# The state tiles' imaginary product: from the vector engine to GpSimd, and its place in GpSimd's queue

## The chip, the cores and the metric

One core of one Trainium2 chip runs the whole program. The metric is the device time of one execution in microseconds, the median of several runs; lower is better. The core has five engines with a queue each: TensorE (PE: matmuls, and PEld for its weight loads), VectorE (DVE), ScalarE (ACT), GpSimd (POOL) and SyncE (SP), which here only issues loads. The engines work in parallel and meet at semaphores. Matmul results go into eight banks of PSUM; everything else the engines share lies in SBUF.

## The reference, cut to what matters

The reference runs two transformer-like blocks of two layers each on 512 positions of width 1024. The change lies in the second block, in the state space part of each layer:

```python
a_bar = jnp.exp(lam * dt)
b_bar = ((a_bar - 1.0) / lam)[..., None] * b_mat
bu = jnp.einsum("bsgh,gph->bsgp", uf.astype(jnp.complex64), b_bar)
...
a_seq = jnp.broadcast_to(a_bar, (1, seq) + a_bar.shape)
_, states = lax.associative_scan(combine, (a_seq, bu), axis=1)
c_mat = lax.complex(c_re.astype(jnp.float32), c_im.astype(jnp.float32))
y = jnp.real(jnp.einsum("bsgp,ghp->bsgh", states, c_mat))
```

There are 16 groups of 64 complex states, so 1024 complex recurrences over 512 positions. Beside it each layer computes a spatial gate, and a differential attention with 4 heads of 2 softmaxes.

## The kernel before, in words

Everything is in float32. The complex recurrence is made real: inputs are turned by the angle of the position so that both parts become plain scans with a real decay, the scans run, and their results are turned back. The 1024 states are eight tiles of 128 partitions, by 512 positions. Turning by an angle takes three multiplications with tables (cos, sin - cos, sin + cos) and a few additions.

For layer `l` and tile `i` the steps are these.

- TensorE, `state_in(i)` (L1221): three products of the layer's input, each into a bank.
- VectorE, `turn_in(i)` (L2531): each bank times a table, into `turned[0..2]`.
- GpSimd (L2030, L2031): `turned[1]` becomes the sum and `turned[2]` the difference with `turned[0]`.
- VectorE, `scan(i)` (L2541, L2543): the scans, into `z_re` and `z_im`.
- GpSimd (L2027): `z_sum = z_re + z_im`.
- VectorE, `turn_out(i)` (L2552, L2553, L2555): `z_re`, `z_im` and `z_sum` times a table each, into `out_parts[1]`, `[2]` and `[0]`. Before it writes, it waits until the product of tile `i - 1`, which reads the same buffers, is in its bank.
- TensorE, `state_out(i)` (L1229): the product of `out_parts` with the output matrices, summed in one bank, called `("yp", l, i)`.
- VectorE, `add_y(i)` (L2499 for tiles 0 and 4, L2504 for the others): adds that bank to the result and so drains it.

Each queue is written out by hand and executed in order. TensorE's holds, for tile `i`: `state_in(i + 1)`, `state_out(i - 1)`, then three steps of the attention (L795 scores, L813 transposes, L825 products with the values). VectorE's holds: `scan(i)`, `turn_in(i + 1)`, in tile 0 the spatial gate (L2577), one attention step (L2201, L2210, L2212, L2218 or L2222), `turn_out(i)`, `add_y(i - 1)`, two more attention steps. GpSimd's holds: L2027 of tile `i`, then L2030 and L2031 of tile `i + 1`. ScalarE has the attention's exponentials and copies (L1486, L1498).

TensorE takes the eight banks in turn, so before it fills one it waits until what was in it eight fills ago is drained; this is how a late `add_y` holds it. SyncE loads tables and matrices of each tile from DRAM into three buffers in turn (L1301, L1303): the load for tile `i + 3` waits until the product of tile `i` is in its bank, and `state_in(i + 3)` waits for the load.

The feed-forward network that follows uses L1786 and L1788 on GpSimd (weights split in two parts), and L2628 and L2083 among others on VectorE.

Of the kernel before, what the change touches and what calls it, by code (L numbers as in the profile page):

```python
# [11 lines left out]
ALU = mybir.AluOpType  # L12
# [33 lines left out]
S5_BUFS = 3  # L46
# [87 lines left out]
def build(nc, A, out, upto=99):  # L134
    ctx = ExitStack()
    with ctx:
# [44 lines left out]
        def region(base, *dims):  # L181
            n = int(np.prod(dims))
            ap = arena[:, base:base + n]
            if len(dims) == 2:
                return ap.rearrange("p (a b) -> p a b", a=dims[0])
            return ap
# [80 lines left out]
        s5_tabs = [region(9216 + 3 * T * b, 3, T) for b in range(S5_BUFS)]  # L267
        mats0 = cst[:, CONST["cosm"][0]:CONST["cosm"][0] + 2 * S5_MATS].rearrange("p (m n) -> p m n", m=6)
        s5_mats = [mats0] + [region(13824 + 2 * S5_MATS * b, 6, P) for b in range(S5_BUFS - 1)]
        z_re, z_im, z_sum = (xnT[:, i, :] for i in range(3))  # L270
        turned = [xnT[:, 3 + i, :] for i in range(3)]
        out_parts = [xnT[:, 6, :], xnT[:, 7, :], region(16128, T)]
# [64 lines left out]
        def s5(name):  # L337
            at, w = S5_AT[name]
            return sp_[:, at:at + w]
# [4 lines left out]
        def S(name):  # L344
            if name not in made:
                made[name] = ctx.enter_context(nc.semaphore(name))
            return made[name]
# [18 lines left out]
        def filled_sem(key):  # L366
            return (over_filled if over(key) else bank_filled)[number[key] % BANKS], number[key] // BANKS + 1

        def bank(key):
            return psum[number[key] % BANKS]  # L370

        def wait_filled(eng, key):
            eng.wait_ge(*filled_sem(key))
            return bank(key)
# [4 lines left out]
        def wait_drained(eng, key):  # L379
            eng.wait_ge(drained_sem(key), number[key] // BANKS + 1)  # L380
# [168 lines left out]
        def _(pe):  # L549
            def claim(key):  # L550

                n = tiles[over(key)]
                tiles[over(key)] += 1
                assert key not in number, key
                number[key] = n
                if n >= BANKS:
                    pe.wait_ge(drained_sem(key), n // BANKS)
                return psum[n % BANKS]

            def fill(ins, key):  # L560
                ins.then_inc(filled_sem(key)[0], 1)
# [603 lines left out]
            with pe.If(n_tokens > CAP):  # L1165
                for i in range(BANKS):
                    n = tiles[False] - 1 - i
# [10 lines left out]
            for l in range(L2):  # L1178
# [45 lines left out]
                def state_out(i):  # L1224

                    ps = claim(("yp", l, i))
                    pe.wait_ge(S("out_parts_ready"), 8 * l + i + 1)
                    for m in range(3):
                        ins = pe.matmul(ps[:, :], s5_mats[i % S5_BUFS][:, 5 - m, :], out_parts[m], start=m == 0,  # L1229
                                        stop=m == 2)  # L1230
                    fill(ins, ("yp", l, i))
# [537 lines left out]
        def _(pool):  # L1769
# [122 lines left out]
            for t in range(NT):  # L1892
                for a in range(2):
                    i = a * NT + t
# [19 lines left out]
            for q in range(S5_ROUNDS):  # L1914
                l = q // 2
# [50 lines left out]
            for l in range(L2):  # L1966
                for half in range(2):
# [5 lines left out]
                    for k in range(9):  # L1973
                        n = 1 << k
# [20 lines left out]
            for a in range(2):  # L1995
                for t in range(NT):
                    i = a * NT + t
# [6 lines left out]
            for l in range(L2):  # L2004

                if l:
                    wait_drained(pool, ("up", f"ffn2_{l - 1}", KF - 1, 1))
                pool.dma_start(wn, A["gmlp_w_s_2"][l].rearrange("h i j -> i h j")).then_inc(S("gmlp_in"), 16)
                pool.dma_start(vgain, A["gmlp_v_g_2"][l:l + 1, :].broadcast_to([P, 256])).then_inc(S("gmlp_in"), 16)
                for i, name in enumerate(("lambda_q1_2", "lambda_k1_2", "lambda_q2_2", "lambda_k2_2")):  # L2010
                    pool.dma_start(lamrow[:, i, :], A[name][l:l + 1, :].broadcast_to([P, 64])).then_inc(S("gmlp_in"), 16)
                pool.dma_start(subg, A["subln_g_2"][l:l + 1, :].broadcast_to([P, P])).then_inc(S("gmlp_in"), 16)
                pool.wait_ge(S("gmlp_in"), 16 * 7 * (l + 1))
                pool.memset(wn[0:64, :, 64:128], 0.0).then_inc(S("wn_ready"), 1)
                if l == 0:
                    pool.wait_ge(S("results_added"), 2 * NT)
                split(f"in{l}")
                split(f"qk{l}", 6)
                rotary(groups2(l), f"g2_{l}", lambda l=l: split(f"qk{l}", 2))

                for i in range(-1, 8):
                    n = 8 * l + i
                    if i >= 0:
                        pool.wait_ge(S("scan_done"), n + 1)
                        if n:
                            pool.wait_ge(S("out_parts_ready"), n)
                        pool.tensor_tensor(z_sum, z_re, z_im, ALU.add).then_inc(S("z_sum_ready"), 1)  # L2027
                    if i < 7:
                        wait_drained(pool, ("bu", l, i + 1, 0))
                        pool.tensor_tensor(turned[1], turned[0], turned[1], ALU.add).then_inc(S("bu_turned"), 1)  # L2030
                        pool.tensor_tensor(turned[2], turned[0], turned[2], ALU.subtract).then_inc(S("bu_turned"), 1)  # L2031

                wait_filled(pool, ("mt", f"m2_{l}", NT - 1, 1))
                pool.wait_ge(S("y_split"), 2 * (l + 1))
                split(f"out2_{l}")
                if upto <= 6 + 2 * l:
                    return
                split(f"ff{l}")
                if upto <= 7 + 2 * l:
                    return  # L2040
# [3 lines left out]
        def _(dve):  # L2044
# [461 lines left out]
            for l in range(L2):  # L2506
# [26 lines left out]
                def scan(i):  # L2533

                    n = 8 * l + i
                    rb = s5("r")[:, n:n + 1].broadcast_to([P, T])
                    if n:
                        dve.wait_ge(S("out_parts_ready"), n)
                        dve.wait_ge(S("z_sum_ready"), n)
                    dve.wait_ge(S("bu_turned"), 2 * n + 1)  # L2540
                    dve.tensor_tensor_scan(z_re, rb, turned[1], 0.0, ALU.mult, ALU.add)  # L2541
                    dve.wait_ge(S("bu_turned"), 2 * n + 2)
                    dve.tensor_tensor_scan(z_im, rb, turned[2], 0.0, ALU.mult, ALU.add).then_inc(S("scan_done"), 1)  # L2543

                def turn_out(i):

                    n = 8 * l + i
                    tabs = s5_tabs[i % S5_BUFS]
                    dve.wait_ge(S("scan_done"), n + 1)
                    if i:  # L2550
                        wait_filled(dve, ("yp", l, i - 1))
                    dve.tensor_tensor(out_parts[1], z_re, tabs[:, 1, :], ALU.mult)  # L2552
                    dve.tensor_tensor(out_parts[2], z_im, tabs[:, 2, :], ALU.mult)  # L2553
                    dve.wait_ge(S("z_sum_ready"), n + 1)
                    dve.tensor_tensor(out_parts[0], z_sum, tabs[:, 0, :], ALU.mult).then_inc(S("out_parts_ready"), 1)  # L2555

# [52 lines left out]
                for j in range(KF):  # L2609
                    n = up2[0]  # L2610
# [55 lines left out]
```

## Time and profile before

| | us |
|---|---|
| median of 3 runs | 3069.35 (3067.13 to 3070.07) |
| the profiled execution | 3073.82 |
| its span, first to last instruction | 3072.0 |
| TensorE busy | 2920.0 (95%) |
| GpSimd busy | 1605.2 (52%) |
| VectorE busy | 1083.7 (35%) |
| ScalarE busy | 709.7 (23%) |

Busy times are averages over stages with different limits. The state tiles take only a small part of the span: those of the first layer lie at about 1843 to 1938 us, those of the second at 2528 to 2618 us. Matmuls overlap, so a busy TensorE is not one at its peak. In lists by time, a row has its start, its length, engine, line, operation, what it writes and reads, and in brackets the idle time of the engine before it with what ended that. A row's length includes a wait of the instruction for anything that the semaphores don't show.

### The profile page before, as it was taken

Reading aid. Unit: us, or ns where it says so; the run is one execution under the profiler, and the core shown is the slowest. Engines: PE = TensorE matmul, PEld = TensorE weight load, DVE = VectorE, ACT = ScalarE, POOL = GpSimd, SP = SyncE. Lnnn points to the kernel's source line nnn. Section 1 sums busy time; section 2 is a strip of 40 time slices with the busy share of each in tenths; the row PEclk is TensorE's granted clock in tenths of the full one; section 3 lists DMA queues with packets and bytes.
Section 4 is the critical chain, followed back from the end, with each engine's and each line's share of the span. In section 5 each row is a group of like instructions: output and inputs, shape, how many; then the busy total and the mean of one; then the engine's idle time right before and its main releaser. Section 6 shows DMA issues by size and latency. Waiting matters only on the chain.

```text
span 3072.0 us, 38813 instructions
## 1 busy us (share of the span) xinstructions
PE 2920.0 (95%) x14757; PEld 2381.5 (78%) x14757; DVE 1083.7 (35%) x2145; ACT 709.7 (23%) x1735; POOL 1605.2 (52%) x1687
## 2 busy tenths in 40 slices
PE   6999999999999899999999898799999988899999
PEld 3545888888878799999999764588888764688887
DVE  1026643313255200000001238447264148357273
ACT  3135752101110111111110222432022222432020
POOL 0121027767778210107784543278788643378786
PEclk9999999999999899999999998899999989899999
DMA  6260013233442389999999303223333203133331
GB/s 184 61 186 25 15 29 97 89 108 95 124 122 91 96 240 265 263 261 267 299 301 309 111 31 114 63 83 93 106 93 106 79 31 136 45 94 96 102 93 52
DMA packets 543191, 388.07 MB, mean 126 GB/s; under 512 B 31178, under 2 KB 493221, under 8 KB 542488
## 3 DMA queue, kind: packets, MB, share of 16 engines
q1 hardware_dynamic: 523728, 327.85, 37.6%
q0 software_dynamic: 12832, 41.22, 4.0%
q10 hardware_dynamic: 6440, 16.44, 1.5%
q8 instruction: 121, 1.98, 0.3%
q14 instruction: 70, 0.57, 0.1%
HBM read 345.12 MB, written 40.80 MB: 126 GB/s over the span
## 4 chain that ended last, share of the span: by engine, by line
PE 88%; DVE 4%; ACT 3%; issue 2%; DMA 1%; SPq 1%; ACTq 1%; POOL 0%; another core or an unknown queue 0%; DVEq 0%; POOLq 0%
PE bank L593 17%; PE bank L594 17%; PE bank L595 17%; PE bank L728 15%; PE bank L1147 6%; PE bank L825 3%; PE bank L795 2%; PE bank L1221 1%; PE bank L813 1%; PE bank L1229 1%; PE bank L782 1%; PE bank L768 1%; DMA ring<-in_moe_w_down 1%; SPq L1286 1%; PE bank L891 1%
## 5 line engine op out<-in xcount | busy, mean ns | idle before, releaser
L1788 POOL TENSOR_TENSOR unit_parts<-ring,unit_parts 128x512 fp32r<-128x512 f32 x580 | 804.2, 1387 | 48.3
L1786 POOL TENSOR_SCALAR unit_parts<-ring 128x512 fp32r<-128x512 f32 x580 | 425.4, 734 | 538.4 <-PE bank L595 322.6
L593 PE MATMUL bank<-x_hi,unit_parts 128*128 128x512 f32 x1408 | 557.0, 396 | 16.5 <-DVE x L2234 10.3
L594 PE MATMUL bank<-x_lo,unit_parts 128*128 128x512 f32 x1408 | 550.6, 391 | 0.0
L595 PE MATMUL bank<-x_hi,unit_parts 128*128 128x512 f32 x1408 | 550.4, 391 | 0.0
L728 PE MATMUL bank<-arena,ring 128*128 128x160 f32 x2816 | 386.6, 300 | 3.5 <-ACT arena L1617 3.5
L728 PEld LDWEIGHTS bank<-arena,ring 128*128 128x128 f32 x2816 | 384.4, 191 | 3.9 <-ACT arena L1617 3.8
L593 PEld LDWEIGHTS bank<-x_hi,unit_parts 128*128 128x128 f32 x1408 | 265.7, 189 | 75.7 <-DVE x L2234 11.5
L593 PE MATMUL bank<-unit_parts,hid_parts 128*128 128x512 f32 x784 | 308.6, 394 | 9.2 <-DVE hid_parts L2256 9.2
L594 PEld LDWEIGHTS bank<-x_lo,unit_parts 128*128 128x128 f32 x1408 | 265.8, 189 | 57.0 <-issue 2.9
L595 PEld LDWEIGHTS bank<-x_hi,unit_parts 128*128 128x128 f32 x1408 | 265.8, 189 | 56.1
L594 PE MATMUL bank<-unit_parts,hid_parts 128*128 128x512 f32 x784 | 306.8, 391 | 0.0
L595 PE MATMUL bank<-unit_parts,hid_parts 128*128 128x512 f32 x784 | 306.7, 391 | 0.0
L2298 DVE TENSOR_TENSOR arena<-bank,arena 128x160 f32<-128x160 f32 x88 | 28.6, 325 | 567.3 <-PE bank L728 561.2
L1887 POOL TENSOR_TENSOR arena<-arena 128x1024 f32<-128x1024 f32 (+9 forms) x48 | 69.7, 1452 | 265.8 <-ACT arena L1662 265.2
L1147 PE MATMUL bank<-arena,ring 128*128 128x160 f32 x1408 | 195.7, 302 | 5.4 <-DMA ring<-in_moe_w_down 5.4
L1147 PEld LDWEIGHTS bank<-arena,ring 128*128 128x128 f32 x1408 | 193.7, 192 | 6.0 <-issue 5.6
L2234 DVE TENSOR_TENSOR x<-bank,x 128x512 f32<-128x512 f32 x80 | 55.2, 690 | 371.0 <-PE bank L595 371.0
L593 PEld LDWEIGHTS bank<-unit_parts,hid_parts 128*128 128x128 f32 x784 | 148.1, 189 | 40.8 <-DVE hid_parts L2256 10.0
L1755 ACT ACTIVATE arena<-arena,vec 128x512 f32<-128x512 f32 x88 | 71.9, 817 | 464.4 <-DVE arena L2616 464.4
L595 PEld LDWEIGHTS bank<-unit_parts,hid_parts 128*128 128x128 f32 x784 | 148.1, 189 | 31.4
L594 PEld LDWEIGHTS bank<-unit_parts,hid_parts 128*128 128x128 f32 x784 | 148.1, 189 | 30.3
(311 smaller groups left out, 3665.2 us busy)
## 6 DMA issues: line engine op xcount, KB each, us to landing
ring<-in_moe_w_gate SPq DMA_DIRECT2D x88, 512.0 KB, 6.6
ring<-in_moe_w_up SPq DMA_DIRECT2D x88, 512.0 KB, 7.3
ring<-in_moe_w_down SPq DMA_DIRECT2D x64, 704.0 KB, 5.6
ring<-in_w_up SPq DMA_DIRECT2D x88, 512.0 KB, 5.1
ring<-in_w_down SPq DMA_DIRECT2D x16, 1024.0 KB, 5.1
ring<-in_od_w_in SPq DMA_DIRECT2D x24, 512.0 KB, 4.8
s_stream<-arena POOLq DMA_DIRECT2D x12, 1024.0 KB, 9.6
arena<-s_stream SPq DMA_DIRECT2D x16, 768.0 KB, 4.3
```

What stands on the lines that cost most here:

```text
L593: pe.matmul(ps, a[0], b[0], start=start, stop=False)
L594: pe.matmul(ps, a[0], b[1], start=False, stop=False)
L595: return pe.matmul(ps, a[1], b[0], start=False, stop=stop)
L728: ins = pe.matmul(ps[rows_at:rows_at + m, 0:n], w[:, k * width + at:k * width + at + m], src[:, k, :], start=k == 0, stop=k == KD - 1)
L795: ins = pe.matmul(ps[:, 0:k.shape[1]], u["q"](t), k, start=k is ks[0], stop=k is ks[-1])
L825: ins = pe.matmul(ps[:, 0:u["vw"]], pT_buf[0:w, j % 2, kt * P:kt * P + P], u["v"](kt, w), start=kt == 0, stop=kt == kts - 1)
L1147: ins = pe.matmul(ps[:, (m - m0) * CAP:(m - m0 + 1) * CAP], w[:, k * P:(k + 1) * P], hidE[:, k, :], start=k == 0, stop=k == KE - 1)
L1755: act.activation(acc[:, 2 * a + n % 2, :], unscaled[:, a, :], ACT.Identity, scale=vcol("conv_w_2", 132 * l + 88 + f), bias=vcol("conv_b_2" ...
L1786: pool.tensor_scalar(hi, raw, 1.0, 1.0, ALU.mult, ALU.mult).then_inc(S("units_rounded"), 1)
L1788: pool.tensor_tensor(lo, raw, hi.bitcast(F32), ALU.subtract).then_inc(S("units_split"), 1)
L1887: tt = lambda o, a, b, op: link(pool.tensor_tensor(o, a, b, op))
L2234: drain(dve.tensor_tensor(xs, ps[:, :], xs, ALU.add), key)
```

## The change

The multiplication of `z_im` by its table leaves VectorE's `turn_out` and goes into GpSimd's queue, between the sum L2027 and the two additions of the next tile. It takes the wait for tile `i - 1`'s product along (VectorE keeps its own). A new semaphore, `im_turned`, counts it. TensorE waits for it before `state_out`, VectorE before the next tile's scan overwrites `z_im`.

```diff
                     ps = claim(("yp", l, i))
                     pe.wait_ge(S("out_parts_ready"), 8 * l + i + 1)
+                    pe.wait_ge(S("im_turned"), 8 * l + i + 1)
...
                         pool.tensor_tensor(z_sum, z_re, z_im, ALU.add).then_inc(S("z_sum_ready"), 1)
+                        if i:
+                            wait_filled(pool, ("yp", l, i - 1))
+                        pool.tensor_tensor(out_parts[2], z_im, s5_tabs[i % S5_BUFS][:, 2, :], ALU.mult)\
+                            .then_inc(S("im_turned"), 1)
...
                         dve.wait_ge(S("z_sum_ready"), n)
+                        dve.wait_ge(S("im_turned"), n)
...
                     dve.tensor_tensor(out_parts[1], z_re, tabs[:, 1, :], ALU.mult)
-                    dve.tensor_tensor(out_parts[2], z_im, tabs[:, 2, :], ALU.mult)
                     dve.wait_ge(S("z_sum_ready"), n + 1)
                     dve.tensor_tensor(out_parts[0], z_sum, tabs[:, 0, :], ALU.mult).then_inc(S("out_parts_ready"), 1)
```

Line numbers of the changed kernel differ. On GpSimd L2027 becomes L2028, the new multiplication is L2031, L2030 and L2031 become L2035 and L2036. On VectorE the scans are L2547 and L2549, `turn_in` L2536, `turn_out` L2558 and L2560, `add_y` L2504 and L2509. TensorE's `state_out` is L1230; `state_in` and the attention keep their lines.

The queue of GpSimd before, tiles 1 and 2 of the first layer (`bank_drained4` is the drain of the first product of the next tile; `xnT` is the buffer that holds the turned and scanned parts):

```order
L2027 TENSOR_TENSOR xnT<-xnT 128x512 [waits out_parts_ready,scan_done]
L2030 TENSOR_TENSOR xnT<-xnT 128x512 [waits bank_drained4]
L2031 TENSOR_TENSOR xnT<-xnT 128x512
L2027 TENSOR_TENSOR xnT<-xnT 128x512 [waits out_parts_ready,scan_done]
L2030 TENSOR_TENSOR xnT<-xnT 128x512 [waits bank_drained0]
L2031 TENSOR_TENSOR xnT<-xnT 128x512
```

and the same two tiles in the changed kernel (`bank_filled7` and `bank_filled3` are the products of tiles 0 and 1):

```order
L2028 TENSOR_TENSOR xnT<-xnT 128x512 [waits out_parts_ready,scan_done]
L2031 TENSOR_TENSOR arena<-xnT,arena 128x512 [waits bank_filled7]
L2035 TENSOR_TENSOR xnT<-xnT 128x512 [waits bank_drained4]
L2036 TENSOR_TENSOR xnT<-xnT 128x512
L2028 TENSOR_TENSOR xnT<-xnT 128x512 [waits out_parts_ready,scan_done]
L2031 TENSOR_TENSOR arena<-xnT,arena 128x512 [waits bank_filled3]
L2035 TENSOR_TENSOR xnT<-xnT 128x512 [waits bank_drained0]
L2036 TENSOR_TENSOR xnT<-xnT 128x512
```

The multiplication and its wait now stand ahead of both additions of the next tile.

The queue of VectorE before, tile 2 of the first layer, from the second scan to the addition of tile 1's product (`bank_filled3` is that product):

```order
L2543 SCALAR_TENSOR_TENSOR xnT<-s5small,xnT 128x512 [waits bu_turned]
...
L2201 ISA arena,small<-bank,cst 128x512 [waits bank_filled4,probs_ready]
L2201 ISA small 128x1
L2222 SCALAR_TENSOR_TENSOR arena<-bank,small,arena 128x128 [waits bank_drained7,bank_filled7]
L2552 TENSOR_TENSOR xnT<-xnT,arena 128x512 [waits bank_filled3,scan_done]
L2553 TENSOR_TENSOR arena<-xnT,arena 128x512
L2555 TENSOR_TENSOR xnT<-xnT,arena 128x512 [waits z_sum_ready]
L2504 TENSOR_TENSOR arena<-arena,bank 128x512 [waits bank_drained7,bank_filled3]
```

and in the changed kernel:

```order
L2549 SCALAR_TENSOR_TENSOR xnT<-s5small,xnT 128x512 [waits bu_turned]
...
L2206 ISA arena,small<-bank,cst 128x512 [waits bank_filled4,probs_ready]
L2206 ISA small 128x1
L2227 SCALAR_TENSOR_TENSOR arena<-bank,small,arena 128x128 [waits bank_drained7,bank_filled7]
L2558 TENSOR_TENSOR xnT<-xnT,arena 128x512 [waits bank_filled3,scan_done]
L2560 TENSOR_TENSOR xnT<-xnT,arena 128x512 [waits z_sum_ready]
L2509 TENSOR_TENSOR arena<-arena,bank 128x512 [waits bank_drained7,bank_filled3]
```

Two operations are left between the attention's step and the addition, and VectorE's own wait for `bank_filled3` stays at the first of them.

## Rows read from the trace of the kernel before

**Rows 1.** The page: the span, and busy time of each engine.
```profile
span 3072.0 us, 38813 instructions
...
PE 2920.0 (95%) x14757; PEld 2381.5 (78%) x14757; DVE 1083.7 (35%) x2145; ACT 709.7 (23%) x1735; POOL 1605.2 (52%) x1687
```

**Rows 2.** Stretch, first layer, tiles 2-7: us; busy PE, PEld, DVE, ACT, POOL; clock; DMA.
```profile
1871.80:1936.60 64.80, 56.03 (x232) 30.91 (x231) 52.77 (x117) 16.47 (x50) 20.12 (x16) 0.95 0.40 142
```

**Rows 3.** The chain of waits in the first layer's tiles: start us, us, what.
```profile
1877.47 0.60 DVE xnT L2555
...
1908.38 6.46 DMA arena<-s_stream
...
1921.79 0.63 PE bank L795 x4
...
1925.17 0.60 DVE xnT L2555
```

**Rows 4.** Groups by line and shape, GpSimd (count, busy us, mean ns).
```profile
L2031 POOL TENSOR_TENSOR xnT<-xnT 128x512 f32<-128x512 f32 x16 | 20.4, 1272 | 0.0
...
L1805 POOL TENSOR_TENSOR arena<-arena,cst 128x512 f32<-128x512 f32 x16 | 17.5, 1092 | 55.8 <-DVE arena L2180 55.8
```

**Rows 5.** The list by time, tile 3 of the first layer.
```profile
1885.65 0.32 SPq L1301 DMA_DIRECT2D arena<-s_stream  x1
...
1887.33 0.83 DVE L2552 TENSOR_TENSOR xnT<-xnT,arena 128x512 f32<-128x512 f32 x1
...
1888.69 0.68 DVE L2555 TENSOR_TENSOR xnT<-xnT,arena 128x512 f32<-128x512 f32 x1
...
1890.02 0.49 PE L825 MATMUL bank<-arena 128*128 128x128 f32 x2 [1.17 <-DVE arena L2504]
...
1890.97 2.84 PE L1221 MATMUL bank<-arena 128*128 128x512 f32 x6 [0.46 <-DMA arena<-s_stream]
```

**Rows 6.** The list by time, tiles 2, 5, 6 and 7 of the first layer.
```profile
1873.93 0.32 SPq L1301 DMA_DIRECT2D arena<-s_stream  x1
...
1876.19 0.68 DVE L2552 TENSOR_TENSOR xnT<-xnT,arena 128x512 f32<-128x512 f32 x1
...
1877.39 0.68 DVE L2555 TENSOR_TENSOR xnT<-xnT,arena 128x512 f32<-128x512 f32 x1
...
1914.88 4.34 PE L1221 MATMUL bank<-arena 128*128 128x512 f32 x6 [1.27 <-DMA arena<-s_stream]
...
1923.88 0.68 DVE L2552 TENSOR_TENSOR xnT<-xnT,arena 128x512 f32<-128x512 f32 x1
...
1925.08 0.68 DVE L2555 TENSOR_TENSOR xnT<-xnT,arena 128x512 f32<-128x512 f32 x1
...
1933.24 0.68 DVE L2552 TENSOR_TENSOR xnT<-xnT,arena 128x512 f32<-128x512 f32 x1
...
1934.44 0.69 DVE L2555 TENSOR_TENSOR xnT<-xnT,arena 128x512 f32<-128x512 f32 x1
```

**Rows 7.** The list by time, GpSimd and VectorE in a feed-forward network.
```profile
2741.31 0.62 POOL L1786 TENSOR_SCALAR unit_parts<-ring 128x512 fp32r<-128x512 f32 x1 [0.20 <-PE bank L595]
...
2747.68 1.60 POOL L1788 TENSOR_TENSOR unit_parts<-ring,unit_parts 128x512 fp32r<-128x512 f32 x1
...
2748.16 1.66 DVE L2628 TENSOR_TENSOR whole<-arena 128x512 f32<-128x512 f32 x1
...
2749.25 1.06 POOL L1786 TENSOR_SCALAR unit_parts<-ring 128x512 fp32r<-128x512 f32 x1
...
2749.75 1.10 DVE L2083 TENSOR_TENSOR hid_parts<-whole,hid_parts 128x512 fp32r<-128x512 f32 x1
```

**Rows 8.** The list by time, second layer: TensorE after tiles 3 and 5.
```profile
2574.14 2.84 PE L1221 MATMUL bank<-arena 128*128 128x512 f32 x6 [0.40 <-DMA arena<-s_stream]
...
2596.62 2.74 PE L1221 MATMUL bank<-arena 128*128 128x512 f32 x6
```

**Rows 9.** Busy times by stretch, first layer behind tile 5.
```profile
1915.00:1917.50 2.50, 2.50 (x3) 1.05 (x4) 1.31 (x2) 0.00 (x0) 1.11 (x1) 0.50 1.04 404
```

## The prediction

> **What bounds the kernel now.** I read the page first. The span is 3072.0 us and TensorE is busy for 95% of it, VectorE for 35%, GpSimd for 52% [rows 1], so an edit on VectorE and GpSimd can only count where TensorE waits for one of them. The edit sits in the two loops over state tiles, eight tiles for each layer of the second block. The busy times by stretch show them: tiles 2 to 7 of the first layer fill 64.80 us, with VectorE busy 52.77 us and TensorE 56.03 us of them [rows 2]. There VectorE is nearly as full as TensorE.
>
> Next comes the chain of waits through this loop [rows 3]. The reader is to see two kinds of link. In some tiles it runs through VectorE: the turning out (L2553, L2555), the addition of the last tile's product (L2504), and then TensorE, which wants the bank that this addition drains. In others it runs through the load of a later tile's tables, which starts when the product of an earlier tile is in its bank (L1229) and takes some 5 us. In the first layer loads end it after tiles 1, 3 and 5, VectorE in tiles 2, 4, 6 and 7; in the second VectorE has tile 5 as well. So VectorE's turning out lies on the path in nine of the sixteen tiles, and just behind it in others.
>
> **What the change removes.** Sixteen VectorE multiplications (L2553). A row of the kind shows 0.68 us, but they follow one another every 0.6 us (L2552 at 1933.24, L2555 two steps later at 1934.44 [rows 6]). If nothing else moved, the nine tiles on VectorE's path would give 9 x 0.6 = 5.4 us.
>
> **What it adds.** Sixteen multiplications of 128x512 on GpSimd. The nearest rows are L1805, the same operation on the same shape with both operands read in full, 1.09 us, and the additions around it, 1.27 us [rows 4]. I take 1.09, since that is a multiplication; successive operations there start some 0.05 us earlier than the row's length, so a step is 1.04 for it and 1.22 for an addition. GpSimd idles most of the loop, so the time itself costs nothing. What matters is where it lands.
>
> Before, GpSimd's three operations of a tile (the sum L2027, then L2030 and L2031 on the next tile) end just before VectorE begins to turn out. The new one waits until the previous tile's product is in its bank, and L2030 and L2031 queue behind it. In tile 3 of the first layer the product is there at 1885.65, when the queue that waits for the same event issues its load [rows 5]. The multiplication then runs 1885.67 to 1886.71, and L2030 and L2031 follow where before they were over at 1887.6. VectorE arrives at L2552 at 1887.33 [rows 5], in the middle of L2030.
>
> **The price of meeting.** In the second layer's feed-forward network VectorE's L2628, both inputs in SBUF, shows 1.66 us where one alone takes about 0.6: it ends 0.54 us after GpSimd's L1788. The GpSimd operation behind it (L1786) shows 1.06 us against about 0.62 undisturbed, and L2083, next on VectorE, 1.10 [rows 7]. So two such operations never run at once, and with both queues full they take turns, one and one. By the Trainium skill (SBUF — State Buffer, who interferes with whom) a VectorE instruction with two SBUF inputs and a GpSimd one that reads SBUF exclude each other for the whole instruction, and whichever comes first goes first; this trace agrees with the exclusion (1.66 us). That rule speaks against this change: without it the sum would be the gain of 5.4 us above, with it the loss below.
>
> **The sum, tile by tile** (first layer, shift of the start of L2555 against its own row).
> - Tile 3: L2552 waits for L2030's end, 1887.93, and runs to 1888.53; now L2031 has its turn, to 1889.75; L2555 starts then, before at 1888.69 [rows 5]. That is +1.06. TensorE waited 0.46 us more for a load here [rows 5], so 0.60 comes through.
> - Tile 2: the product is there at 1873.93, L2552 is ready at 1876.19 and finds L2030 just ending; it runs to 1876.84, L2031 to 1878.06; L2555 before 1877.39 [rows 6]. +0.67, all on the path.
> - Tiles 4 and 5: taken as tile 3, whose pattern they repeat, +1.06. Tile 4 has no load behind it and passes all on. After tile 5 TensorE waits 1.27 us for a load anyway [rows 6]: 0.
> - Tile 6: the product comes late, at 1921.79, when TensorE goes on to L795 [rows 3]. L2552, ready at 1923.88, runs from 1924.07 to 1924.67, L2031 to 1925.90, L2555 before 1925.08 [rows 6]: +0.82.
> - Tile 7: nothing follows the multiplication on GpSimd, and it is over when L2552 starts at 1933.24. L2555 loses the step before it: -0.60.
> - Tiles 0 and 1: 0. In tile 0 TensorE's slow matmuls hide it, in tile 1 a load does, and L2555 moves by -0.2 at most.
>
> First layer: 0.67 + 0.60 + 1.06 + 0 + 0.82 - 0.60 = +2.55 us. The second layer repeats the pattern. Its waits differ in two places: 0.40 us for the load after tile 3, and none after tile 5 [rows 8]. 0.67 + 0.66 + 1.06 + 1.06 + 0.82 - 0.60 = +3.67. Together +6.2 us.
>
> Edits that cost nothing. TensorE's new wait for the multiplication precedes a matmul that comes a whole tile, 10 us, later. VectorE's new wait before the scan is met by then too. L2031 of tile 3 ends at 1889.75 and its reader, the scan of tile 4, starts at 1891.5 or later. That cover of over 1.7 us is what the loop would lose first if the queue grew. The load queue waits for the same banks as before.
>
> **The clock.** Longer waits of TensorE can drop its clock. After the load wait of 1.27 us behind tile 5 it was granted 0.50 (1.2 of 2.4 GHz) in 1915.0 to 1917.5, and L1221 showed 4.34 us instead of the 2.84 of tile 3 [rows 5, 6, 9]: +1.5 us. The waits of tile 3, 1.17 us for VectorE and 0.46 for a load, did not bring a fall: L1221 behind them shows 2.84. The change stretches the waits for VectorE in tiles 2 to 4 of both layers, six of them, by 0.7 to 1.1 us, to about 2. Between no fall and six (0 to +9.0) I take two, +3.0: that lies nearer to the row of tile 3, which brought none, and part of a slow stretch can fall into a wait and cost nothing.
>
> Sum against the profiled execution: 3072.0 + 6.2 + 3.0 = 3081.2 us of span. That execution took 3073.82 us, 4.5 above the median of the three runs, 3069.35. The same difference on the median gives 3078.6 us.
>
> **Rivals.**
> - *VectorE keeps its place.* If its two turning operations ran back to back in spite of GpSimd waiting, L2555 would lose no turn: it would start 0.6 us after L2552: 1876.84 against 1877.39 is -0.55 in tile 2, 1888.53 against 1888.69 is -0.16 in tiles 3 to 5, 1924.67 against 1925.08 is -0.41 in tile 6, and -0.60 in tile 7. On the path that makes -0.55 - 0.16 - 0.41 - 0.60 = -1.7 us in the first layer and -1.9 in the second (tile 5 too): 3065.7. For it speaks that the two have nothing between them. Against it stands the turn-taking of rows 7, where L2083 was next in line and still let L1786 through.
> - *The relief counts and the meeting does not*, the other side. If the two queues only seldom met, because the additions were early or the wait for the bank ended earlier, the nine tiles on the path would keep their 0.6: 3069.35 - 5.4 = 3064.0. The point of decision is whether L2030 has ended when L2552 is ready; by the rows it has not in tiles 3, 4 and 6.
> - *The clock falls every time.* 3069.35 + 6.2 + 9.0 = 3084.6. For it speaks the fall behind tile 5; against it, that the new waits stand alone, with busy stretches between.
> - *The queue reaches the scan.* If L2031 ended over 1.7 us later than worked out, the scan of the next tile would wait and everything with it, about 1 us in each of 12 tiles: 3069.35 + 6.2 + 12 = 3087.6. The rows leave room.
>
> **How the numbers follow.** About 0.2%, 6.1 us, is what a measurement of this kernel can tell from no change. Forecast (turns taken, none to three falls, 3075.5 to 3080.1) 0.58; every or nearly every fall 0.14; VectorE keeps its place 0.14; relief 0.10; scan reached 0.04. The forecast's low end, +6.2 without any fall, lies at the bound, so a fifth of it counts as the same. Slower by over 0.2%: 0.46 + 0.14 + 0.04 = 0.64. Same: 0.12 + 0.14 + most of relief (-5.4 is inside the bound) 0.06 = 0.32. Faster: 0.04. The range leaves out the relief and the scan's case: 3065.5 to 3086.5 us.
>
> **What would show it.** Right: sixteen rows of the new L2031 on GpSimd near 1.09 us, starting as the product's bank fills; L2558 often longer than 0.68 us; L2036 with rows of about 1.9 us, having waited a turn; L2560 over 1.2 us after L2558 in tiles 2 to 6; TensorE's waits for L2509 longer by about 1 us. Wrong: L2560 0.6 us behind L2558 throughout, which is the first rival, or TensorE's waits for it shorter than before, which is the second. Any wait of L2547 for GpSimd would show the last rival. Were the clock's term wrong, the loop alone would say so: its granted clock against 0.95 in tiles 2 to 7 [rows 2].

## The result and the profile after

The changed kernel takes 3088.2 us in the median of 5 runs (3086.66 to 3094.16), the kernel before 3070.07 (3067.13 to 3074.57): a ratio of 1.0061, 95% interval 1.0049 to 1.0074. It is slower by some 18 us. The forecast had the sign and not the size: 3078.6, with a range that ended at 3086.5. The profiled execution took 3086.96 us.

The page of the changed kernel, against [rows 1]: 13.1 us more span, and GpSimd busy 25.9 us more. VectorE gave away sixteen multiplications and is busy 5.0 us longer all the same. The last row is TensorE's granted clock in 40 slices of the span, 77 us each. The two loops lie at slices 24 to 26 and 33 to 35; six slices show 8 there, where the kernel before has four.

```profile
span 3085.1 us, 38828 instructions
...
PE 2929.3 (95%) x14757; PEld 2387.7 (77%) x14757; DVE 1088.7 (35%) x2129; ACT 710.1 (23%) x1735; POOL 1631.1 (53%) x1703
...
PEclk9999999999999899999999988899999988899999
```

Tile 3 of the first layer, listed by time, against [rows 5]:

```profile
1884.47 0.32 SPq L1302 DMA_DIRECT2D arena<-s_stream  x1
1884.53 1.27 POOL L2031 TENSOR_TENSOR arena<-xnT,arena 128x512 f32<-128x512 f32 x1 [1.84 <-PE bank L1230]
...
1885.75 1.28 POOL L2035 TENSOR_TENSOR xnT<-xnT 128x512 f32<-128x512 f32 x1
...
1886.15 1.42 DVE L2558 TENSOR_TENSOR xnT<-xnT,arena 128x512 f32<-128x512 f32 x1
...
1886.97 1.72 POOL L2036 TENSOR_TENSOR xnT<-xnT 128x512 f32<-128x512 f32 x1
...
1887.50 1.75 DVE L2560 TENSOR_TENSOR xnT<-xnT,arena 128x512 f32<-128x512 f32 x1
...
1889.16 0.67 DVE L2509 TENSOR_TENSOR arena<-arena,bank 128x512 f32<-128x512 f32 x1
...
1889.89 0.72 PE L825 MATMUL bank<-arena 128*128 128x128 f32 x2 [2.23 <-DVE arena L2509]
...
1890.41 4.24 PE L1221 MATMUL bank<-arena 128*128 128x512 f32 x6
```

This is the meeting that was forecast. GpSimd's three operations start as the product's bank fills. VectorE's first (L2558) holds on until L2035 is over, GpSimd's L2036 until L2558 is over, VectorE's second (L2560) until L2036 is over, and the waits stand as length in the rows: 1.42, 1.72 and 1.75 us for work of 0.6, 1.2 and 0.6. From the queue's load to the end of `turn_out`'s last operation it was 1889.37 - 1885.65 = 3.72 us before, and is 1889.25 - 1884.47 = 4.78 now: +1.06, as worked out. TensorE's wait went from 1.17 to 2.23 us.

What comes behind the wait is the other part. The same six matmuls of L1221 took 2.84 us before and take 4.24 now. Stretches of tile 3 in the changed kernel (us; busy PE, PEld, DVE, ACT, POOL; clock; DMA):

```profile
1885.00:1890.00 5.00, 2.77 (x22) 2.08 (x21) 4.12 (x5) 1.23 (x4) 3.70 (x3) 1.00 0.67 236
1890.00:1892.50 2.50, 2.50 (x5) 1.42 (x6) 2.43 (x10) 1.25 (x5) 0.00 (x0) 0.50 0.00 0
1892.50:1895.00 2.50, 2.50 (x6) 0.99 (x5) 1.44 (x3) 0.00 (x0) 1.23 (x1) 0.82 0.00 0
```

The clock falls to its lower level, 1.2 GHz, as TensorE comes back from its wait, and has risen again before the last stretch ends. Much the same happens in tiles 1 to 6 of both layers. TensorE's rows behind its waits, first layer, tiles 1, 2, 4, 5, 6 and 7 in turn:

```profile
1863.02 1.22 PE L825 MATMUL bank<-arena 128*128 128x128 f32 x4 [2.29 <-DVE arena L2504]
1864.03 3.83 PE L1221 MATMUL bank<-arena,cst 128*128 128x512 f32 x6
1875.89 0.48 PE L795 MATMUL bank<-arena 64*128 64x128 f32 x2 [1.86 <-DVE arena L2509]
1878.49 3.37 PE L1221 MATMUL bank<-arena 128*128 128x512 f32 x6
...
1902.67 1.13 PE L795 MATMUL bank<-arena 64*128 64x512 f32 x2 [1.88 <-DVE arena L2509]
1905.28 3.63 PE L1221 MATMUL bank<-arena,cst 128*128 128x512 f32 x6
1916.99 1.82 PE L825 MATMUL bank<-arena 128*128 128x128 f32 x8 [2.38 <-DVE arena L2504]
1918.61 3.79 PE L1221 MATMUL bank<-arena 128*128 128x512 f32 x6
1930.43 1.16 PE L795 MATMUL bank<-arena 64*128 64x384 f32 x2 [2.50 <-DVE arena L2509]
1939.63 0.60 PE L825 MATMUL bank<-arena 128*128 128x128 f32 x3 [0.52 <-DVE arena L2509]
```

Before, L1221 showed 2.84, 2.74, 2.84, 2.74 and 4.34 us behind the waits of tiles 1 to 5, so one of five was slow; now all five are. Behind tile 6 none follows, but L795 takes 1.16 us for 0.91 before. And no wait for a load is left: all are for `add_y`.

For the sum over both loops I take the time from the start of the scan of tile 0 to that of tile 7 in each layer. Before and after (columns as above):

```profile
1847.49:1928.23 80.74, 69.50 (x275) 40.08 (x275) 68.46 (x158) 18.59 (x60) 26.38 (x21) 0.90 0.36 129
2529.15:2608.83 79.68, 69.22 (x271) 40.18 (x271) 68.46 (x158) 18.80 (x60) 26.38 (x21) 0.89 0.37 131
```

```profile
1842.56:1932.93 90.37, 75.98 (x271) 44.47 (x271) 71.30 (x150) 18.91 (x60) 37.99 (x28) 0.82 0.32 115
2532.01:2622.40 90.39, 75.96 (x271) 44.44 (x271) 71.30 (x151) 18.91 (x60) 38.01 (x28) 0.82 0.33 115
```

Together 160.4 us before and 180.8 after, +20.3; with tile 7's turning out, which lost its multiplication, the loops grew by 19.1 us. They hold the whole loss. TensorE is busy 13.2 us more in them with the same matmuls, and that is the clock, not the wait: idle time does not count as busy.

### The profile page after: what moved, and what is told of

Same layout as the page of the kernel before. It is cut to its first block, busy times and chain, and to the rows that moved or that the text cites. A ratio compares the mean times of both kernels' runs of the same rounds, so it can differ in the third digit from the quotient of the medians.

```text
span 3085.1 us, 38828 instructions
## 1 busy us (share of the span) xinstructions
PE 2929.3 (95%) x14757; PEld 2387.7 (77%) x14757; DVE 1088.7 (35%) x2129; ACT 710.1 (23%) x1735; POOL 1631.1 (53%) x1703
## 4 chain that ended last, share of the span: by engine, by line
PE 88%; DVE 4%; ACT 3%; issue 2%; DMA 1%; SPq 1%; ACTq 0%; POOL 0%; another core or an unknown queue 0%; DVEq 0%; POOLq 0%
PE bank L593 17%; PE bank L595 17%; PE bank L594 17%; PE bank L728 15%; PE bank L1147 6%; PE bank L825 3%; PE bank L795 2%; PE bank L1221 2%; PE bank L813 1%; PE bank L1230 1%; PE bank L782 1%; PE bank L768 1%; DMA ring<-in_moe_w_down 1%; SPq L1287 1%; DVE xnT L2560 1%
## 6 DMA issues: line engine op xcount, KB each, us to landing
s_stream<-arena POOLq DMA_DIRECT2D x12, 1024.0 KB, 10.1
```

## The experiments

All were timed beside the kernel before, and each ratio is to its time there (3070.8 to 3072.5 us in the median on the experiments' chips, 3070.07 beside the changed kernel). "Loops" is the sum of the two stretches just defined, "clock" the granted clock from the scan of tile 2 to that of tile 7, first and second layer, both from one profiled execution.

| kernel | median us | ratio (95%) | loops us | clock |
|---|---|---|---|---|
| before | 3070.8 to 3072.5 | 1 | 160.4 | 0.97, 0.98 |
| changed | 3088.20 | 1.0061 (1.0049 to 1.0074) | 180.8 | 0.88, 0.88 |
| e1 two buffers | 3073.09 | 0.9997 (0.9984 to 1.0009) | 158.7 | 0.98, 0.94 |
| e2 last in the queue | 3084.48 | 1.0036 (1.0023 to 1.0049) | 170.5 | 0.94, 0.90 |
| e3 longer VectorE | 3105.91 | 1.0099 (1.0083 to 1.0114) | 189.7 | 0.86, 0.86 |
| e4 changed, filled | 3074.76 | 1.0005 (0.9997 to 1.0014) | 164.4 | 1.00, 1.00 |
| e5 relief alone | 3063.66 | 0.9977 (0.9965 to 0.9989) | 156.8 | 0.95, 0.98 |
| e6 addition alone | 3102.17 | 1.0101 (1.0082 to 1.0119) | 195.6 | 0.85, 0.85 |
| e7 before, filled | 3063.27 | 0.9971 (0.9959 to 0.9983) | 156.5 | 1.00, 1.00 |
| e8 two buffers, filled | 3060.28 | 0.9964 (0.9954 to 0.9975) | 154.3 | 1.00, 1.00 |
| e9 longer VectorE, filled | 3083.23 | 1.0036 (1.0024 to 1.0049) | 170.5 | 1.00, 1.00 |
| e10 changed, half filled | 3076.59 | 1.0011 (0.9998 to 1.0023) | 164.8 | 1.00, 0.99 |
| e11 two buffers, filled more | 3067.40 | 0.9983 (0.9971 to 0.9995) | 154.9 | 1.00, 1.00 |

What lies outside the loops differs from execution to execution: the first scan starts anywhere from 1840.4 us (e4) to 1850.9 (e11), in kernels that are alike up to there. So the loops of one execution say more of a mechanism than the medians do, and the intervals bound what the medians say. How often the clock falls is read from one execution of each kernel too. The granted clock of the whole span, known for every timed execution, goes the same way: in the mean 0.970 for the kernel before, 0.968 for the changed one, 0.969 for e1 and e2, 0.971 for e5, 0.964 and 0.965 for e3 and e6, 0.972 to 0.974 for the six filled ones.

**e1, the meeting taken away.** Two buffers for the imaginary part, so that GpSimd multiplies right behind its sum, long before VectorE's turning out. `state_out` reads the two in turn (not shown here).

```diff
+        im_parts = [region(16128, T), region(16640, T)]
...
-                        if i:
-                            wait_filled(pool, ("yp", l, i - 1))
-                        pool.tensor_tensor(out_parts[2], z_im, ..., ALU.mult)
+                        if i >= 2:
+                            wait_filled(pool, ("yp", l, i - 2))
+                        pool.tensor_tensor(im_parts[i % 2], z_im, ..., ALU.mult)
```

> The changed kernel with two buffers for the imaginary product, so that GpSimd's multiplication follows its sum at once and does not wait for the last tile's product. Theory A (the loss is the place: GpSimd's additions pushed into VectorE's turning out, which then gives up turns, and TensorE's clock behind the longer waits): the three operations of GpSimd end at most 0.5 us later than before, L2560 starts as in the kernel before or 0.6 us sooner, granted clock in tiles 2 to 7 back near 0.95; 3066 to 3070 us, ratio to the kernel before 0.999 to 1.000. Rival B (the work on GpSimd itself costs, wherever it stands): still some 18 us slower, ratio 1.005 to 1.006.

3073.09 us, 0.9997: the 18 us are gone, as expected. VectorE's two operations follow each other in 0.6 us (tile 2, first layer), and TensorE's wait is 0.64 us where it was 1.24 before and 1.86 in the changed kernel:

```profile
1877.71 0.68 DVE L2559 TENSOR_TENSOR xnT<-xnT,arena 128x512 f32<-128x512 f32 x1
1878.31 0.69 DVE L2561 TENSOR_TENSOR xnT<-xnT,arena 128x512 f32<-128x512 f32 x1
1878.91 0.68 DVE L2510 TENSOR_TENSOR arena<-arena,bank 128x512 f32<-128x512 f32 x1
1879.64 0.48 PE L796 MATMUL bank<-arena 64*128 64x128 f32 x2 [0.64 <-DVE arena L2510]
```

So the loss hangs on where GpSimd's work lands, not on its amount and not on the new semaphore, which both stayed. The relief brings little against the kernel before here: 1.7 us in the loops.

**e2, behind both additions.** The multiplication and its wait moved behind GpSimd's L2035 and L2036 of the changed kernel; the same lines leave their old place (not shown here).

```diff
                         pool.tensor_tensor(turned[2], turned[0], turned[2], ALU.subtract).then_inc(S("bu_turned"), 1)
+                        if i:
+                            wait_filled(pool, ("yp", l, i - 1))
+                        pool.tensor_tensor(out_parts[2], z_im, ..., ALU.mult).then_inc(S("im_turned"), 1)
```

> The changed kernel with GpSimd's multiplication, and its wait for the last tile's product, behind both additions of the next tile. Theory A: the additions end as before, but the multiplication itself now meets the turning out: one turn of 1.2 us between the two VectorE operations, less the 0.6 saved: about +0.7 us in tiles 2 to 6 (5 us in all), and part of the clock's cost; 3077 to 3084 us, ratio 1.002 to 1.005. Rival C (the harm is the additions arriving late for the next scan, not the meeting): back to 3064 to 3070 us.

1.0036, inside what was expected. VectorE's two operations now meet one GpSimd operation, the multiplication, where they met two; TensorE's wait in tile 3 is 1.64 us, between the 1.17 of before and the 2.23 of the changed kernel, and half of what the loops had lost stays (10.1 of 20.3 us). That the additions come late for the next scan, the rival here, is out: they are back in their place and the kernel is still slower.

**e3, only VectorE's work made longer.** The kernel before, with `turn_out`'s second multiplication issued three times, twice into buffers that nobody reads. GpSimd's queue is as before.

```diff
                     dve.tensor_tensor(out_parts[2], z_im, tabs[:, 2, :], ALU.mult)
+                    for at in (16640, 15360)[:2]:
+                        dve.tensor_tensor(region(at, T), z_im, tabs[:, 2, :], ALU.mult)
```

> The kernel before, with two more multiplications of z_im into scratch on VectorE in each turning out (1.2 us per tile), GpSimd untouched. It lengthens TensorE's wait for VectorE in tiles 2 to 6 by the same 1 us or so as the change, without any meeting. Clock theory (a longer wait lowers TensorE's clock, whatever makes it): about +13 us of waits on the path and +9 to +12 us of slower matmuls: 3090 to 3096 us, granted clock in tiles 2 to 7 near 0.88, L1221 3.4 to 4.3 us in place of 2.8. Rival (the clock fell for another reason, such as GpSimd's traffic): +13 us only, 3083 us, clock stays near 0.95.

3105.91 us, more than either theory had. It shows without GpSimd's part that a later `add_y` alone brings the clock down (0.86) and costs more than the work that delays it: 1.2 us of VectorE's work for each of twelve waiting tiles are 14.4 us, and the loops grew by 29.3.

**e4, the changed kernel with its waits filled.** TensorE's wait for the bank comes first; what is filled is the wait for `add_y` one claim later, with products of the identity with itself in the bank that is about to be used and is overwritten after.

```diff
+            key_at = {}
...
                 if n >= BANKS:
                     pe.wait_ge(drained_sem(key), n // BANKS)
+                key_at[n] = key
+                late = key_at.get(n + 1 - BANKS, ("",))
+                if late[0] == "yp":
+                    for _ in range(8 if late[2] in (1, 3, 5) else 6 if late[2] in (0, 2, 4) else 0):
+                        pe.matmul(psum[n % BANKS][:, 0:P], c("ident"), c("ident"), start=True, stop=True)
                 return psum[n % BANKS]
```

> The changed kernel, with TensorE kept busy where it waits for VectorE's addition: in the bank claimed just before that wait it multiplies the identity by itself, 8 times in tiles 2, 4 and 6 and 6 times in tiles 1, 3 and 5 (1.3 to 1.8 us), before the real products overwrite it. Clock theory: granted clock in tiles 2 to 7 over 0.95, L1221 back to 2.7 to 2.9 us, time 8 to 12 us under the changed kernel: 3076 to 3080 us. Rival (the slower clock costs nothing, the matmuls would wait anyway): 3088 us or more, since the added products delay some real ones.

3074.76 us, better than expected: 8 to 12 us under the changed kernel were forecast, and by the ratios (1.0005 against 1.0061) it is some 17. This separates the two parts of the loss, since VectorE and GpSimd do just what they do in the changed kernel. They still take turns (tile 3):

```profile
1882.35 1.72 POOL L2043 TENSOR_TENSOR xnT<-xnT 128x512 f32<-128x512 f32 x1
1882.76 1.50 PE L564 MATMUL bank<-cst 128*128 128x128 f32 x12
1882.86 1.75 DVE L2567 TENSOR_TENSOR xnT<-xnT,arena 128x512 f32<-128x512 f32 x1
...
1885.26 0.49 PE L832 MATMUL bank<-arena 128*128 128x128 f32 x2 [0.89 <-DVE arena L2516]
1885.59 2.74 PE L1228 MATMUL bank<-arena 128*128 128x512 f32 x6
```

L564 is the filling. `add_y` comes as late as ever (the turning out ends 4.77 us after the load queue's issue at 1879.84, in the changed kernel 4.78), but `state_in` (L1228 here) is back at 2.74 us, and the loops are 16.4 us shorter than the changed kernel's. Work that computes nothing gave the time back.

**e5, the relief alone.** The kernel before without VectorE's multiplication. The imaginary part of the state outputs is left out of the computation; its buffer is zeroed once per layer.

```diff
-                    dve.tensor_tensor(out_parts[2], z_im, tabs[:, 2, :], ALU.mult)
```

> The kernel before with VectorE's multiplication of the imaginary part left out and nothing put in its place; its buffer is zeroed once per layer, so the imaginary part of the state outputs is left out of the computation. It prices the relief alone. By the sum of the prediction nine tiles on VectorE's path give 0.6 us each: -5.4 us, ratio 0.998 (3066 to 3068 where the kernel before takes 3072.5). If the clock's loss grows with the length of TensorE's waits, as the larger-than-expected loss of the longer turning out (+33 us for +19 us of VectorE work) suggests, shorter waits also give back some of the slow matmuls of tiles 0 and 5: -7 to -11 us, ratio 0.9965 to 0.998. Rival, that loads end the waits wherever VectorE does not: -1 to -3 us, ratio 0.9990 to 0.9997.

0.9977, -7.1 us on the ratio, with -3.6 in the loops and some -1.2 more in the two last tiles. The prediction's -5.4 lies between; the case in which loads take over everywhere (-1 to -3) is out by the ratio's interval.

**e6, the addition alone.** The kernel before keeps VectorE's multiplication and gets GpSimd's too, into a spare buffer, with the waits of the change.

```diff
                         pool.tensor_tensor(z_sum, z_re, z_im, ALU.add).then_inc(S("z_sum_ready"), 1)
+                        if i:
+                            wait_filled(pool, ("yp", l, i - 1))
+                        pool.tensor_tensor(region(16640, T), z_im, ..., ALU.mult).then_inc(S("im_turned"), 1)
```

> The kernel before, VectorE's multiplication kept, with GpSimd's new multiplication added at the place and with the waits of the change, into a buffer that nobody reads. It prices what the change adds, without its relief. Turns: VectorE has three operations where the changed kernel has two, so its last one ends some 0.6 us later than there, about 1.7 us later than before in tiles 2 to 6; as the clock falls with such waits (the changed kernel lost 16 us to it at +1.1 us per tile), the time is beyond the changed kernel's: +24 to +34 us, ratio 1.008 to 1.011. If the meeting costs nothing and the change's loss came from elsewhere (the moved buffer, the new waits of TensorE alone), this kernel is at 1.000 to 1.002.

1.0101, inside the range for turns. Tile 3, in which GpSimd's multiplication started at 1890.42:

```profile
1892.05 1.41 DVE L2558 TENSOR_TENSOR xnT<-xnT,arena 128x512 f32<-128x512 f32 x1
...
1893.38 1.75 DVE L2559 TENSOR_TENSOR arena<-xnT,arena 128x512 f32<-128x512 f32 x1
1895.05 0.68 DVE L2561 TENSOR_TENSOR xnT<-xnT,arena 128x512 f32<-128x512 f32 x1
```

The turning out ends 5.31 us after that start, in the changed kernel 4.72 us after it (1884.53 to 1889.25): the multiplication that VectorE kept, 0.59 us. So the change as a whole is an addition that costs more and a relief that gives some of it back. The two do not simply add up: without GpSimd's addition the relief is worth 3.6 us of loops (e5), with it 195.6 - 180.8 = 14.8, twice the 7.2 of VectorE's work in twelve tiles, since the clock comes up with it (0.85 to 0.88).

**e7 and e8, the kernel before and e1 filled.** The filling of e4 with five and four products instead of eight and six, once in the kernel before and once in e1.

> The kernel before, with idle multiplications of TensorE (five for odd tiles, four for even, identity by identity into a bank that is claimed already) ahead of each of its waits for the addition of tiles 0 to 5. Clock theory: the kernel before loses something to the clock too (L1221 4.34 behind tile 5, 4.73 in tile 0), and filling the waits gives part of it back: -2 to -6 us, ratio 0.998 to 0.9995, granted clock of the loops 0.99 to 1.00. If the fillers help only by hiding something else in the changed kernel, or cost what they give, 1.000 to 1.001 here.

> The changed kernel with two buffers for the imaginary part (GpSimd's multiplication right behind its sum, ahead of the meeting) and TensorE's waits filled as in the run on the kernel before. The candidate that should beat both kernels. With two buffers alone the ratio was 0.9997 and the granted clock of the loops 0.98 and 0.94; with the clock at 1.00, 3 to 6 us of slower matmuls go: ratio 0.998 to 0.999, 3066 to 3069 where the kernel before takes 3072.5. If the two repairs do not add up, 0.9995 to 1.0005.

Both came out better than expected: 0.9971 and 0.9964, with the clock at 1.00. The kernel before had been losing to its clock too, 3.9 us of its loops (its four falls are told of below). e8 beats both kernels, by 10.5 us and by about 28; the two repairs add up in the loops (-1.7 from the buffers, -3.9 from the filling, -6.1 together). That medians gain 4 to 5 us more than the loops is not explained; such a part is within what executions differ by outside of them.

**e9, e3 filled.** Eleven and ten products.

> The run with the longer turning out on VectorE (ratio 1.0099 without filling, loops at a granted clock of 0.86) with TensorE's waits filled as well: eleven idle multiplications for odd tiles, ten for even, 0.25 us each, about as long as its waits of 3 us. It splits that kernel's loss into waits and clock. Its TensorE was busy 8.0 us longer than before in tiles 2 to 7 of each layer. If that is the clock's doing, filling gives 16 us back: 1.004 to 1.006, granted clock 1.00 in the loops. If the loss is VectorE's work alone, with TensorE's slow rows hidden beside it, it stays at 1.009 to 1.010.

1.0036 against 1.0099, more given back than expected. Of e3's loops 189.7 - 170.5 = 19.2 us were clock, and 170.5 - 156.5 = 14.0 the longer work itself when both are at full clock, close to the 14.4 of twelve tiles at 1.2.

**e10, the changed kernel half filled.** Four and three products.

> The changed kernel with half the filling: four idle multiplications for odd tiles and three for even, about 1.0 and 0.75 us of waits of 1.9 to 2.5. Full filling gave 1.0005, none 1.0061. If the clock's loss falls in proportion to the idle time that is left, 1.003 to 1.0035; if what counts is whether the idle time that is left is about as short as that of the kernel before (0.8 to 1.3 us, which cost it little), most comes back: 1.0005 to 1.002, granted clock of the loops over 0.96. If half the filling brings nothing, 1.005 to 1.006.

1.0011. The return is not proportional: half the filling does what the whole one did (loops 164.8 against 164.4). In tile 3 of this kernel 0.83 us are filled and 1.56 us of the wait are left, and the clock stays up:

```profile
1890.84 0.83 PE L564 MATMUL bank<-cst 128*128 128x128 f32 x6
...
1893.35 0.49 PE L832 MATMUL bank<-arena 128*128 128x128 f32 x2 [1.56 <-DVE arena L2516]
1893.67 2.74 PE L1228 MATMUL bank<-arena 128*128 128x512 f32 x6
```

**e11, e8 filled more.** Seven and six products.

> The best kernel so far (two buffers, filled by five and four, ratio 0.9964) with seven and six, 1.75 and 1.5 us, longer than most of its waits. If fillers past the wait's length delay TensorE, 0.3 to 0.5 us in each of twelve tiles, minus what loads end anyway: ratio 0.9970 to 0.9985. If the wait for the addition is longer than the records show, or the clock has something left to give, it stays at 0.996 to 0.9968.

0.9983, in the range for a delay, but the loops do not bear it out: 154.9 us against 154.3 of e8, where a delay in every tile would be 4 to 6. The two intervals touch (0.9971 to 0.9995, 0.9954 to 0.9975). Whether more filling costs anything stays open; it brings nothing. The profiled execution of e11 came to its first scan 8.4 us later than that of e8, ahead of any filling.

## Why the prediction was wrong in size, point by point

- **GpSimd's multiplication**, taken as 1.09 us: 1.27 in all sixteen rows, like the additions. It cost the sum nothing: in tile 3 the turns still end 4.78 us after the bank is filled, as worked out, since the turns behind it were shorter than taken: 0.54 us for L2558 (0.60), 1.12 for L2036 (1.22), 0.56 for L2560 (0.68).
- **The turns, tile by tile**: right. TensorE's waits in the first layer grew by 1.86 - 1.24 = 0.62 in tile 2 (0.67 forecast), 1.06 in tile 3 (1.06), 1.88 - 0.82 = 1.06 in tile 4 (1.06), 2.50 - 1.67 = 0.83 in tile 6 (0.82). To price them without the clock, compare the filled kernels: e4 - e7 = 164.4 - 156.5 = 7.9 us of loops. The forecast's terms without tile 7's, which lies behind the stretch, are 3.15 + 4.27 = 7.4. Tile 5 agrees as well: 1.33 + 1.27 us of waits became 2.38 in the first layer (0 forecast), 1.33 became 2.38 in the second (1.06). By the Trainium skill (SBUF — State Buffer, who interferes with whom) the two kinds of instruction exclude each other for their whole length; rows of 1.72 and 1.75 us for 1.2 and 0.6 us of work agree again.
- **The count of tiles on VectorE's path**: nine was one short. In the second layer no load ends the wait of tile 1; the chain runs through L2555 (2548.53, 0.60 us) and L2499 to L825 there too (its row stands below), which makes ten tiles and a relief of 6.0 us. It changes the forecast by 0.2 us at most, since the meeting moves tile 1 by no more.
- **The clock: the step that failed.** It is "I take two, +3.0". The changed kernel lost 180.8 - 164.4 = 16.4 us to its clock and the kernel before 160.4 - 156.5 = 3.9, so the change added 12.5 us. I had counted six waits that might fall, and two that would: tiles 1 to 6 of both layers, twelve waits, all have a slow stretch. They are not all alike, L1221 shows 3.37 to 4.26 us for 2.74, and a slow stretch also holds rows of L825 (1.22 us behind tile 1 for 0.71 in e4), which I had not counted. The highest price I gave, +9.0 for six falls at 1.5, was too low for the same reasons. The falls do not go with longer waits alone: tile 1's wait got shorter, from 2.47 to 2.29 and 2.30 us, and has a slow stretch in both layers now, where it had one before.
- **Where the reading went wrong**: I took the fall behind tile 5 [rows 6, 9] for the only one and for the effect of a single wait of 1.27 us, and tile 3's wait of 1.17 as proof that others are harmless. I looked at L1221 alone. Behind tile 6 no L1221 follows, and there the kernel before falls too, after one wait of 1.67 us for `add_y`, in both layers (clock 0.50 here, 0.53 in the second); and behind tile 5 it was two waits. List by time, the last two rows from tile 1 of the second layer, then a stretch behind tile 6 of the first:

```profile
1912.44 1.16 PE L825 MATMUL bank<-arena 128*128 128x128 f32 x8 [1.33 <-DVE arena L2499]
1914.88 4.34 PE L1221 MATMUL bank<-arena 128*128 128x512 f32 x6 [1.27 <-DMA arena<-s_stream]
...
1926.42 0.91 PE L795 MATMUL bank<-arena 64*128 64x384 f32 x2 [1.67 <-DVE arena L2504]
...
2549.84 1.23 PE L825 MATMUL bank<-arena 128*128 128x128 f32 x4 [2.47 <-DVE arena L2499]
2550.86 3.71 PE L1221 MATMUL bank<-arena,cst 128*128 128x512 f32 x6
```

```profile
1928.90:1931.40 2.50, 2.50 (x4) 1.01 (x3) 2.46 (x6) 0.00 (x0) 0.77 (x1) 0.50 0.00 0
```

  With the second layer's tile 1 (a wait of 2.47 us, L1221 3.71) the kernel before had four falls in twelve tiles. Its waits up to 1.33 us, where alone, brought none; those of 1.67 and 2.47 us brought one in three cases of four. The change put all twelve at 1.86 or more. So the trace of before held the warning, in rows behind waits that I did not read; how many falls the change would bring it did not tell, as the last section shows.
- **The rivals.** VectorE does not keep its place: L2560 shows 1.75 us. The relief is real (e5) and outweighed (e6). No scan waited for GpSimd's queue. "The clock falls every time" was the right case with too small a price, 3084.6 against 3088.2, and I gave it 0.14.
- **Loads**: the 0.46 us behind tile 3 and the 1.27 behind tile 5 that ended TensorE's waits before are gone, since the tiles are longer and the loads are not.

## What to carry to other kernels

Before moving work to an idle engine, ask what it meets there: here GpSimd was half idle, and the move cost 8 us of turns because its slot fell on VectorE's own. Of a TensorE that waits, read the row behind the wait too: a wait that grows from 1.2 to 2.2 us may cost its own microsecond and as much again in slow matmuls. Where such a wait can't be removed, three or four idle products in it (0.8 to 1.1 us) gave back 16.0 of the 20.3 us that the loops had lost here, and four or five gave 3.9 us of the loops in a kernel that did not look as if it had a clock problem.

## What the runs showed of the hardware that was not expected

- Waits of 1.86 to 2.50 us, one to a tile of some 13 us, took the granted clock of the loop from 0.97 to 0.88. By the Trainium skill (TensorE: Matmul & The Clock Gate, A second HAM failure mode: psum-queue depth-cycling) idle times of TensorE between groups of matmuls can make the clock swing again and again; this trace agrees (0.50 in 1890.0 to 1892.5, and between any two of a layer's six slow stretches it is back at 1.00).
- The length of a wait does not decide alone. In e2 TensorE waited 2.93 us behind tile 1 and kept its clock, while 1.64 us behind tile 3 was followed by 4.54 us for L1221:

```profile
1865.42 0.71 PE L825 MATMUL bank<-arena 128*128 128x128 f32 x4 [2.93 <-DVE arena L2505]
1865.97 2.74 PE L1221 MATMUL bank<-arena,cst 128*128 128x512 f32 x6
...
1890.27 0.49 PE L825 MATMUL bank<-arena 128*128 128x128 f32 x2 [1.64 <-DVE arena L2510]
1890.75 4.54 PE L1221 MATMUL bank<-arena 128*128 128x512 f32 x6
```

  In the second layer of the same execution it is the other way round: 2.92 us behind tile 1 was followed by 5.17 us for L1221, 1.64 us behind tile 3 by 2.77. And short waits are not safe either. In the second layer of e1 the clock fell behind a wait of 0.80 us (L796 is the L795 of the kernel before, which took 1.12 us there behind 0.82; second line a stretch, columns as above):

```profile
2580.78 1.75 PE L796 MATMUL bank<-arena 64*128 64x512 f32 x2 [0.80 <-DVE arena L2510]
2581.00:2583.50 2.50, 2.50 (x7) 1.11 (x7) 1.40 (x7) 0.74 (x3) 0.00 (x0) 0.53 0.05 14
```

  What else decides, these runs don't tell.
- The clock's loss reaches VectorE: `turn_in` waits for the slow `state_in`. From the loops' start to their end VectorE waited for L1221 13.4 us in the changed kernel and 4.5 in e4, 14.0 in e3 and 0.9 in e9 (both layers together). Whether this makes the next `add_y` later, so that one fall brings on the next, is not shown.
